# z and four of five convolved groups in units of 256 channels over the whole depth, three bank pairs as their homes, and seven of these units' low parts on GpSimd

## The reference, cut to what matters

```
h = rmsnorm(x, norm1_w[l])
proj = jnp.einsum('bsd,dp->bsp', h, w_in[l])
(aq, ak, av, z, xbc, dt_raw, m_qk, m_v, m_o, m_i, m_f) = split_columns(proj, PROJ_SIZES)
...
xbc = jax.nn.silu(causal_dwconv(xbc, conv_w, conv_b)).astype(jnp.float32)
...
y = y.reshape(bsz, seq, SSM_WIDTH) * jax.nn.silu(z.astype(jnp.float32))
...
x = x + jnp.einsum('bsm,md->bsd', mix, w_out[l])
h = rmsnorm(x, norm2_w[l])
x = x + conv_glu(h, ffn_w_up[l], ffn_conv_w[l], ffn_conv_b[l], ffn_w_down[l])
```

## Time and profile before

| | |
|---|---|
| median of 3 runs | 413.14 us (413.11 to 413.23) |
| the profiled execution | 413.05 us, its span 411.3 us |
| PE busy | 406.0 us, 99% of the span |
| DVE, ACT, POOL busy | 304.2, 259.9, 39.3 us |
| DVE, ACT in 18.01 to 72.48 us (units 1 to 9) | 47.18, 40.49 us of 54.47 |
| granted TensorE clock | 1.00 |

### The profile page before, as it was taken

How to read it: one execution, slowest core, us unless ns; L and a number is a source line. 1 busy time by engine, 2 the same in 40 slices (tenths; PEclk the granted TensorE clock), 3 DMA queues, 4 the chain that set the end, 5 groups by cost and what they waited for, 6 DMA issues and landing times.

```text
span 411.3 us, 6393 instructions
## 1 busy us (share of the span) xinstructions
PE 406.0 (99%) x2464; PEld 357.0 (87%) x2464; DVE 304.2 (74%) x434; ACT 259.9 (63%) x351; POOL 39.3 (10%) x27
## 2 busy tenths in 40 slices
PE   8999999999999999999999999999999999999996
PEld 7999999888888899888888888888888888888885
DVE  4988798747756897679867688877677767776775
ACT  5778877795399765997536665654555555535640
POOL 3132544411011000000004000000000000000000
PEclk9999999999999999999999999999999999999999
DMA  8844793475473522225654446646556554455202
GB/s 304 338 162 165 295 329 137 155 211 188 164 257 102 207 102 104 104 102 206 204 204 137 154 147 238 219 158 215 178 191 204 191 214 171 143 206 196 104 0 102
DMA packets 12637, 74.12 MB, mean 180 GB/s; under 512 B 1332, under 2 KB 2760, under 8 KB 4424
## 3 DMA queue, kind: packets, MB, share of 16 engines
q1 hardware_dynamic: 12616, 73.83, 50.4%
HBM read 72.75 MB, written 1.07 MB: 179 GB/s over the span
## 4 chain that ended last, share of the span: by engine, by line
PE 98%; DMA 1%; DVE 0%; POOL 0%; issue 0%; ACT 0%; DVEq 0%; POOLq 0%; ACTq 0%
PE pj L1794 17%; PE pj L1358 13%; PE pj L1360 13%; PE pj L1359 13%; PE pj L1795 10%; PE mx L1359 6%; PE mx L1360 6%; PE mx L1358 6%; PE mx L1408 6%; PE mx L1405 3%; PE pj L1797 2%; DMA x_pad<-in_x 1%; PE pj L1461 0%; PE pj L1457 0%; PE pj L1453 0%; POOL rdiag L369 0%
## 5 line engine op out<-in xcount | busy, mean ns | idle before, releaser
L826 DVE TENSOR_TENSOR wlo<-w_b,whi 128x2048 fp32r<-128x2048 f32 x57 | 130.5, 2290 | 47.3 <-ACT whi L414 47.3
L414 ACT CAST whi<-w_b 128x2048 fp32r<-128x2048 f32 x63 | 120.1, 1908 | 34.8 <-PE pj L1360 29.3
L1794 PE MATMUL pj<-hT,whi 128*128 128x512 f32 x308 | 108.7, 395 | 0.0
L1795 PE MATMUL pj<-hT,wlo 128*128 128x256 f32 x352 | 95.0, 280 | 0.0
L1794 PEld LDWEIGHTS pj<-hT,whi 128*128 128x128 f32 x308 | 57.8, 188 | 12.9
L1795 PEld LDWEIGHTS pj<-hT,wlo 128*128 128x128 f32 x352 | 66.4, 189 | 1.9
L1358 PE MATMUL pj<-hT,whi 128*128 128x256 f32 x208 | 59.3, 285 | 0.0
L1360 PE MATMUL pj<-hT,wlo 128*128 128x256 f32 x208 | 58.9, 283 | 0.0
L1359 PE MATMUL pj<-hT,whi 128*128 128x256 f32 x208 | 58.9, 283 | 0.0
L1358 PEld LDWEIGHTS pj<-hT,whi 128*128 128x128 f32 x208 | 39.7, 191 | 0.3 <-issue 0.3
L378 POOL TENSOR_TENSOR wlo<-w_b,whi 128x2048 fp32r<-128x2048 f32 x6 | 28.1, 4688 | 123.4 <-ACT whi L414 123.4
(11 more groups left out here) (264 smaller groups left out, 628.2 us busy)
## 6 DMA issues: line engine op xcount, KB each, us to landing
w_b<-in_w_in SPq DMA_DIRECT2D x23, 1024.0 KB, 5.0
w_b<-in_w_up SPq DMA_DIRECT2D x22, 1024.0 KB, 4.8
w_b<-in_w_down SPq DMA_DIRECT2D x11, 1024.0 KB, 4.8
w_b<-in_w_out SPq DMA_DIRECT2D x8, 1024.0 KB, 4.8
seg_b<-ld_rows SPq DMA_DIRECT2D x4, 512.0 KB, 6.4
x_pad<-in_x SPq DMA_DIRECT2D x2, 512.0 KB, 3.7
w_b<-in_w0c SPq DMA_DIRECT2D x1, 512.0 KB, 6.1
Wm_b<-m_rows_d SPq DMA_DIRECT2D x1, 512.0 KB, 5.7
```

Source lines behind the costliest of these rows:

```text
L414: nc.scalar.copy(whi[:, slot, :], wraw[:, slot, :]).then_inc(s.hi_done, 1)
L826: nc.vector.tensor_tensor(wlo[:, slot, :], wraw[:, slot, :], whi[:, slot, :].bitcast(F32), ALU.subtract).then_inc(s.lo_done, 1)
L1794: nc.tensor.matmul(ps, whi[:, slot, w], hT[:, k, :, :], start=k == 0, stop=False, skip_group_check=True)
L1795: ins = nc.tensor.matmul(ps[:, 0:T], wlo[:, slot, w], hT[:, k, 0, :], start=False, stop=False, skip_group_check=True)
```

## The change

Groups 1 to 4 and z are cut differently: unit u holds 256 channels over all 8 slices of the depth, as in the FFN, and runs as `pairs` (the FFN's `up` under a new name, with the home as an argument). Its sums have a high half and a low half (the latter hT_lo's share), so each such unit gets two steps more: ACT copies the low half (`conv_low` to so_b, `z_low` to szT), DVE adds it (`conv_sum` in PSUM, `z_sum` in szT). The silu of z is then one instruction a group, out of szT. The homes of units 3 to 9 are pj[0], pj[1] and mx[1], and each unit waits for the taps of the unit that had its home (`freed`). The small columns' turn moves to pj[0], the turned x to mx[0] in two steps. The order of the jobs is written anew: on ACT the softplus stands behind the rounding of unit 3; on DVE the scans stand behind the sum of unit 3, at u = 4. POOL makes the low parts of units 3 to 9, 10 and 12 (before: 4, 6, 8, 10 and 12), DVE no longer those of 3, 5, 7 and 9. The arrays on the host are laid out to match.

```diff
-    POOL_UNITS = (4, 6, 8, 10, 12, U_FFN + 1)
+    POOL_UNITS = (3, 4, 5, 6, 7, 8, 9, 10, 12, U_FFN + 1)
...
+        def conv_home(u):
+
+            return pj[0] if u in (4, 9) else mx[1] if u in (3, 6, 8) else pj[1]
...
+            def conv_low(u):
+
+                act.wait_ge(s.unit_done, u + 1)
+                if u >= 4:
+                    act.wait_ge(s.conv_sum, u - 3)
+                nc.scalar.copy(conv_half(u), part_of(conv_home(u), 1)).then_inc(s.conv_low, 1)
...
-            at(0, rows_softplus)
-            for g in range(NCONV):
-                for b in range(2):
-                    at(2 * g + 2, conv_base, g, b)
-            for g in range(NCONV):
-                for b in range(2):
-                    at(2 * g + 3, conv_act, g, b)
-            at(3, rows_exps)
+            at(1, rows_softplus)
+            for b in range(2):
+                at(2, conv_base, 0, b)
+            for u in range(2, 2 * NCONV):
+                first_at(u + 1, conv_low, u)
+                if u == 4:
+                    at(u + 1, rows_exps)
+                if u == 2:
+                    at(u + 1, conv_act, 0, 0)
+                at(u + 1, conv_base, u // 2, u % 2)
+                at(u + 1, conv_act, (u - 1) // 2, (u - 1) % 2)
+            at(11, conv_act, NCONV - 1, 1)
...
+            at(21, z_low, 0)
...
-            first_at(22, z_evac, 0)
-            first_at(22, pT_copy, 2)
+            first_at(22, z_low, 1)
+            at(22, pT_copy, 2)
+            at(22, exp_table)
+            at(22, z_low, 2)
...
-            at(23, z_table)
-            at(23, z_evac, 1)
+            at(23, z_low, 3)
...
+            at(23, z_table)
+            at(23, z_silu, 0)
...
+            at(24, z_silu, 1)
...
+            def conv_sum(u):
+
+                dve.wait_ge(s.conv_low, u - 1)
+                hi = part_of(conv_home(u), 0)
+                nc.vector.tensor_tensor(hi, hi, conv_half(u), ALU.add).then_inc(s.conv_sum, 1)
...
-            for g in range(NCONV):
-                for b in range(2):
-                    at(2 * g + 2, conv_taps, g, b)
-            at(2, rows_scans)
-            at(3, rows_dec)
-            at(5, cols_copy)
...
+            at(2, conv_taps, 0, 0)
+            first_at(3, conv_sum, 2)
+            at(3, conv_taps, 0, 1)
+            at(3, conv_taps, 1, 0)
+            first_at(4, conv_sum, 3)
+            at(4, rows_scans)
+            at(4, conv_taps, 1, 1)
+            first_at(5, conv_sum, 4)
+            at(5, rows_dec)
+            at(5, conv_taps, 2, 0)
+            first_at(6, conv_sum, 5)
+            at(6, conv_taps, 2, 1)
+            first_at(7, conv_sum, 6)
+            at(7, cols_copy)
+            at(7, xs_evac, 0, 0)
+            at(7, xs_evac, 0, 1)
+            at(7, conv_taps, 3, 0)
+            at(7, skip, 0)
...
-            at(4, cols_turn)
-            at(6, xs_turn)
+            at(6, cols_turn)
+            at(6, xs_turn, 0)
+            at(8, xs_turn, 1)
...
+            freed = {4: 1, 5: 2, 6: 3, 7: 5, 8: 6, 9: 4}
+
             for u in range(U_OUT):
                 g, half = divmod(u, 2)
-                if half == 0 and g >= 2:
+                if u >= U_Z + NT:
+                    pe.wait_ge(s.z_sum, u - U_Z - 1)
+                elif u >= U_Z:
+                    pe.wait_ge(*read_by[G_Z - NT + u - U_Z])
+                elif u in freed:
+                    pe.wait_ge(s.conv_done, freed[u] + 1)
+                    if u == 9:
+                        pe.wait_ge(s.cols_ready, 3)
+                elif half == 0 and g >= NCONV:
                     pe.wait_ge(*read_by[g - 2])
```

More of the change, by code:

```diff
@@ L548, in exp_table, with z_low, z_silu @@
                 nc.scalar.preload_act_table(ACT.Exp)
[L550 to L555, removed]
+            def z_low(i):
+                act.wait_ge(s.unit_done, U_Z + i + 1)
+                nc.scalar.copy(szT[:, 2 * i:2 * i + 2, :], high(i % 2, 1)).then_inc(s.z_low, 1)
+            def z_silu(g):
+                act.wait_ge(s.z_sum, 2 * g + 2)
+                nc.scalar.activation(szT[:, 4 * g:4 * g + 4, :], szT[:, 4 * g:4 * g + 4, :], ACT.Silu).then_inc(s.z_ready, 1)
             def p_exp(h):
@@ L1101, in _ @@
             at(0, rows_softplus)
-            for g in range(NCONV):
-                for b in range(2):
-                    at(2 * g + 2, conv_taps, g, b)
-            at(2, rows_scans)
-            at(3, rows_dec)
-            at(5, cols_copy)
-            for c in range(NT):
-                for half in range(2):
-                    at(7 + 2 * c, xs_evac, c, half)
-                at(7 + 2 * c, skip, c)
+            at(2, conv_taps, 0, 0)
[16 more added lines that the diff above has]
+            at(7, skip, 0)
+            first_at(8, conv_sum, 7)
+            at(8, conv_taps, 3, 1)
+            first_at(9, conv_sum, 8)
+            first_at(9, xs_evac, 1, 0)
+            first_at(9, xs_evac, 1, 1)
+            at(9, conv_taps, 4, 0)
+            at(9, skip, 1)
+            first_at(10, conv_sum, 9)
+            at(10, conv_taps, 4, 1)
             at(12, inter_evac)
@@ L1147, in _ @@
             at(22, p_mask, 7)
+            at(22, z_sum, 3)
             at(22, att_lo, 1)
@@ L1387, in tokens_first, with pairs @@
                 return ins
+            def pairs(home, slot, ks, turned=None):
+                for k in ks:
+                    if turned:
+                        pe.wait_ge(turned, k + 1)
+                    for j in range(2):
+                        w = slice(k * 256 + j * P, k * 256 + (j + 1) * P)
+                        ps = home[:, j * 512:(j + 1) * 512]
+                        if k < KD - 1:
+                            nc.tensor.matmul(ps, whi[:, slot, w], hT[:, k, :, :], start=k == 0, stop=False, skip_group_check=True)
+                        ins = nc.tensor.matmul(ps[:, 0:T], wlo[:, slot, w], hT[:, k, 0, :], start=False, stop=False, skip_group_check=True)
+                        if k == KD - 1:
+                            ins = nc.tensor.matmul(ps, whi[:, slot, w], hT[:, k, :, :], start=False, stop=True, skip_group_check=True)
+                return ins
             def rows_times_pair(dst, a_hi, a_lo, slot, first, last, ready=None, z_read=False, ffn=False):
@@ L1707, in _ @@
                     channels_first(pj[0], u, half, s.lo_T, s.w1_lo).then_inc(s.unit_done, 1)
+                elif u < 2 * NCONV:
+                    pairs(conv_home(u), u % NR, range(KD)).then_inc(s.unit_done, 1)
+                elif u >= U_Z:
+                    pairs(pj[u % 2], u % NR, range(KD)).then_inc(s.unit_done, 1)
                 else:
-                    kind(pj[g % 2], u % NR, half).then_inc(s.unit_done, 1)
+                    tokens_first(pj[g % 2], u % NR, half).then_inc(s.unit_done, 1)
                 for job, args in jobs.get(u, []):
@@ L1783, in down @@
                                 slot, first, last, ffn=True).then_inc(s.unit_done, 1)
-            def up(h, slot, ks, turned=None):
-                for k in ks:
-                    if turned:
-                        pe.wait_ge(turned, k + 1)
-                    for j in range(2):
-                        w = slice(k * 256 + j * P, k * 256 + (j + 1) * P)
-                        ps = pj[h][:, j * 512:(j + 1) * 512]
-                        if k < KD - 1:
-                            nc.tensor.matmul(ps, whi[:, slot, w], hT[:, k, :, :], start=k == 0, stop=False, skip_group_check=True)
-                        ins = nc.tensor.matmul(ps[:, 0:T], wlo[:, slot, w], hT[:, k, 0, :], start=False, stop=False, skip_group_check=True)
-                        if k == KD - 1:
-                            ins = nc.tensor.matmul(ps, whi[:, slot, w], hT[:, k, :, :], start=False, stop=True, skip_group_check=True)
-                return ins
             pe.wait_ge(s.x2_ready, 2 * NT - 1)
@@ L1806, in _ @@
             lo_ready(pe, U_FFN + 1)
[L1807 to L1809 removed]
+            pairs(pj[1], (U_FFN + 1) % NR, first)
+            pairs(pj[0], U_FFN % NR, rest, s.h2_lo).then_inc(s.unit_done, 1)
+            pairs(pj[1], (U_FFN + 1) % NR, rest).then_inc(s.unit_done, 1)
             def step(i, b, first=False, last=False):
```

87 lines of the change are left out of this document (52 added, 35 removed).

## The result

The changed kernel takes **423.13 us** (median of 5 runs, 423.05 to 423.24), the kernel before 413.14 (5 runs, 413.11 to 413.23): 1.024 times as long, 95% interval 1.023 to 1.0252. The prediction said 422.5, in 414 to 427. The profiled execution took 423.17 us.

The account below looks back on a forecast made before the run. PE, 98% of the chain and never waiting after 7 us, was taken as the bound. Waits of +10.8 and a gain of -2.4 gave +8.4; with +0.9 for the clock, 413.05 became 422.4, the median 422.5 us, range 414 to 427.

Parts of the forecast that it names:

- The likeliest case: POOL's low parts stop DVE's scans twice, after one stop in the softplus: 419.5 to 427 us, chance 0.57.
- wait of unit 4: PE waits before unit 4 for the taps of unit 1, late behind the stopped softplus: +1.3 us.
- wait of unit 6: PE waits before unit 6 for the taps of unit 3, late behind the twice-stopped scans: +7.0 us.
- wait of unit 7: PE waits before unit 7 for the taps of unit 5, which end at 63.8 us: +2.1 us.
- the walk: The new order followed instruction by instruction through units 1 to 9 with profiled durations; unit 10 begins at 83.0 us.
- the clock's term: After idling 7 us before unit 6, PE may return at the lower clock: 0 to +1.9 us, +0.9 taken.
- The port's price: A DVE instruction contending for SBUF behind a POOL low part waits until it ends, up to 4.62 us.
- The rival of sharing: DVE and POOL share, or low parts are not in DVE's way; softplus and scans undelayed: 411.9 us, chance 0.20.
- The softplus stopped at line 857: POOL's low part of unit 3 holds DVE's softplus from 21.3 to 25.2 us; its end moves from 25.3 to 29.1.
- The scans stopped twice: POOL's units 6 and 7 hold DVE's scans until 43.9 and 49.3 us; the scans end at 51.9.
- The rival with one stop: POOL's unit 7 comes behind the scans or lets them through; unit 6 waits 2.5 us: 417.0 us, chance 0.20.
- The gain: On PE, 0.2 us for each of 12 shorter units: 1.6 us in units 2 to 9, 0.8 in z, -2.4 us.

Follow-up runs that it names:

- Experiment 4: The changed kernel with dummy matmuls filling PE's waits ahead of units 4 (8 of them) and 6 (26): 423.95 us.
- experiment 1: The kernel before with unit 5's low part moved from DVE to POOL as well: 415.38 us (one run).
- experiment 2: The changed kernel with the low parts of units 6 and 7 back on DVE, so POOL is out of the scans: 417.38 us.
- experiment 3: The changed kernel with the low part of unit 3 alone back on DVE, so POOL is out of the softplus: 421.21 us.
- experiment 5: The changed kernel with the low parts of units 3, 6 and 7 back on DVE: 416.12 us.
- experiment 6: The changed kernel with each POOL low part made of four instructions of 512 columns instead of one: 420.52 us.
- experiment 9: The kernel before with only z and groups 3 and 4 (units 6 to 9) in units of 256 channels, and unit 11's low part also on POOL: 411.87 us.

## Why the prediction was right, point by point

The likeliest case came true: a stop in the softplus, two in the scans. Its terms, up to unit 10, the waits by the pitch:

| term | predicted | measured |
|---|---|---|
| eight shorter units, 2 to 9 | -1.6 | -1.1 |
| wait of unit 4 | 1.3 | 2.1 |
| clock in unit 4 | none | 1.65 |
| wait of unit 6 | 7.0 | 5.2 |
| clock in unit 6 | 0.9 | 2.0 |
| wait of unit 7 | 2.1 | 0.4 |
| wait of unit 8 | 0.4 | 0.3 |
| turns | 0 | -0.1 |
| start of unit 10, from 73.51 | 83.9 | 83.94 |

The predicted start is the walk's 83.0 and the clock's 0.9; its terms add up to 83.6, so the walk's own date is 0.3 too late for them. The measured column adds up to 83.96. The sum is right to 0.4 us and the parts are not. Most of their cancelling is no luck: **DVE's chain sets the dates**, not PE's. It ends the scans (51.9 predicted, 52.5 measured) and the taps of unit 5 (63.8 and 64.65), and PE begins unit 7 at 64.70, right behind them. What PE loses ahead of that, as a wait or as slow matmuls, comes out of the same time. Experiment 4 shows it: with the clock up, the time lost moved to unit 7.

The last 0.9 us, from the clock's term, is luck. By the walk a slow unit 6 would have ended inside the 2.1 us that unit 7 had to wait, so the clock's 0.9 should not have been added to the waits. It made up for DVE's chain being 0.85 late at the taps of unit 5, of which 0.7 was there from the end of the softplus on (29.8 for 29.1), by the later landing of unit 3's load.

- **The port's price** (the wait lasts until POOL's instruction ends): right in each place, by the ends of three instructions above and by experiments 1 to 3, 5 and 6. The rival of sharing, 411.9 us, is out: in units 3 to 9 no instruction of DVE with all operands in SBUF got through beside a low part. Over all eleven profiled executions 25 such instructions began inside a low part of POOL or a piece of one (at least 0.2 us before its end) and 24 were held to its end; the one that was not, a scan of experiment 4 at 45.09 us, came 0.03 us behind POOL's start of 45.06, and there POOL's instruction took 4.79 us instead of 4.6. Of 588 with an operand in PSUM none took over 0.15 us longer than elsewhere, small ones included (4x256 in 0.48 us, in experiment 6), so it is where the operands lie and not the size that decides. By the rule of the Trainium skill (SBUF — State Buffer, "Who interferes with whom"), whoever issues first has the shared pair for the whole instruction; the traces here agree, with 4.38 us for an instruction of 0.33, and with pieces 1.04 to 1.44.
- **The softplus stopped at line 857** (895 in the changed kernel): right, though POOL began a microsecond later than in the walk (21.34 for 20.4), because the load of unit 3 landed at 19.33 and not at 18.4. So the wait of unit 4 was 2.1 instead of 1.3. Which instruction is caught follows this date, which differs by 2 us between executions: in experiment 2 (landed at 17.96) it was one two places ahead, in experiment 4 (19.94) the next one, at 23.85.
- **The scans stopped twice**: right, by units 6 and 7, the first and the eighth instruction where the walk had the first and the fourth: unit 4 ended at 44.32 instead of 41.9, so unit 7 came to POOL at 46.99 instead of 44.5. By experiment 4 this shift moves no date behind the scans. The rival with one stop, 417.0, is out by the two rows; experiment 2 has such a time for another reason, DVE's two low parts more.
- **The clock's term** is the one that was mis-sized: 0.9 predicted, 3.65 measured in two units, of which unit 4's wasn't thought of, for a wait of 1.3 us had been given none. By experiment 4 none of it reached the start of unit 7, for the reason above; in experiment 5 the same fall behind unit 7's wait, the last one of weight, costs 1.2. By the Trainium skill (TensorE: Matmul & The Clock Gate, Part 1) the clock drops to 1.2 GHz when PE has been idle; the trace agrees for the wait of 5 us, while in unit 4 the fall came 1.5 us after PE was back at work.
- **The wait of unit 7** was 0.4 instead of 2.1: unit 6 was slow by 2.0.
- **The gain**: 0.16 us a unit and not 0.2, and a little less behind a wait (units 7 and 8 take 5.74 and 5.76 us, unit 9 5.64). z gave 0.66 in the changed kernel, 0.63 by itself, with 0.8 predicted; that its copies and sums are hidden was right.

The change has a gain of 1.8 us in it (1.1 in units 2 to 9, 0.66 in z), which the waits hide: experiment 9 has two thirds of its units in the new form and is 1.26 us faster than before. Of the loss of 10.0 us, 7.0 come from low parts on POOL that meet the softplus and the scans (experiment 5; 8.2 where its clock stays up). The rest is read from the waits and not isolated by a run: the order and DVE's load leave the chain of sum, base and taps no slack at units 6 and 7, and the clock falls behind that wait. Whether an order exists in which units 2 to 5 gain too was not tried.

## What to carry to other kernels

A low share of busy time on GpSimd is no room: before work is given to it, look at what DVE does in that time. In these traces DVE instructions whose operands are all in SBUF, down to one of a single element, wait for the whole GpSimd instruction (24 of 25); those with an operand in PSUM don't (588). A chain of small dependent instructions is the worst neighbour, because it is stopped again by each low part that begins in a gap of it, and cutting the long instruction only spreads the wait. And when a stretch is bound by another engine than PE, don't add PE's slow clock to its waits: ask for the date that the other engine sets, and whether the slow unit moves it.

## What the hardware did that was not expected

- After a wait of PE of only 2 us the clock fell to the lower level, 1.5 us after PE had begun again, for about 3.5 us (1.65 us lost in unit 4). In experiment 5 the same happened behind a wait of 2.3 us; by the mean granted clock it did in three of four executions, at 416.1 us, and in the fourth not, at 414.97. In experiment 2, with waits of 1.4 and 2.3 us, the mean granted clock was 1.0 in two executions and 0.991 and 0.995 in two, 1.5 to 2.3 us apart.
- A scan, a sum of one element on 4 partitions and an instruction over 16 partitions last 4.71, 4.37 and 4.94 us, nearly the same: each began 0.14 to 0.21 us behind POOL's low part and had almost all of it ahead.
- An instruction of DVE stopped by POOL ended up to 0.55 us behind POOL's own end in the records (26.49 for 25.94), in other places 0.01 (51.57 for 51.56). The difference is the stopped instruction's own time, 0.68 and 0.15 us, less 0.13 and 0.14.
